# The last down projection of a two-layer encoder step, with tokens as the stationary side of the matmul

## What is computed

```python
def _swiglu(h, wg, wu, wd):
    return (jax.nn.silu(h @ wg) * (h @ wu)) @ wd
...
        h = _rmsnorm(x, prm['ffn_norm'][i, 1])
        x = x + 0.5 * _swiglu(h, prm['ffn_w_gate'][i, 1], prm['ffn_w_up'][i, 1], prm['ffn_w_down'][i, 1])
```

## Time and profile before

| what | value |
|---|---|
| median of 3 runs | 1389.95 us (1389.91 to 1391.57) |
| the profiled execution | 1391.69 us, its span 1390.0 us, mean granted clock 0.998 |
| TensorE with matmuls in flight | 1370.0 us (99%), 10726 matmuls |
| VectorE, ScalarE, GpSimd busy | 865.0 us (62%), 584.2 us (42%), 335.1 us (24%) |
| DMA | 188.34 MB, mean 136 GB/s |

### The profile page before, as it was taken

One profiled execution on the slowest core, in us unless ns is written; L12 is line 12 of the kernel. 1 busy time (PEld: TensorE's weight loads), 2 busy tenths in 40 slices (PEclk: granted clock), 3 DMA queues, 4 the chain that ended last, 5 costly groups with the idle time before them and its releaser, 6 DMA issues.

```text
span 1390.0 us, 27392 instructions
## 1 busy us (share of the span) xinstructions
PE 1370.0 (99%) x10726; PEld 1333.7 (96%) x10726; DVE 865.0 (62%) x1397; ACT 584.2 (42%) x1061; POOL 335.1 (24%) x352
## 2 busy tenths in 40 slices
PE   9999999999999999999999999999999899999998
PEld 8999999999879999999999999998999799999998
DVE  6666646577786666655666655667663667666542
ACT  6333323434765333323433332368544544333321
POOL 4000013766426000022100002456755240000000
PEclk9999999999999999999999999999999999999999
DMA  7655962434522655854455594233333225555661
GB/s 200 183 148 150 275 173 54 120 117 130 160 70 70 173 150 146 224 153 103 124 149 150 151 257 128 60 101 92 93 92 92 91 69 149 151 151 154 166 164 38
DMA packets 324067, 188.34 MB, mean 136 GB/s; under 512 B 10986, under 2 KB 321384, under 8 KB 323996
## 3 DMA queue, kind: packets, MB, share of 16 engines
q1 hardware_dynamic: 322416, 183.23, 48.3%
q0 software_dynamic: 1216, 3.98, 0.9%
q10 hardware_dynamic: 364, 0.15, 0.0%
HBM read 183.22 MB, written 4.11 MB: 135 GB/s over the span
## 4 chain that ended last, share of the span: by engine, by line
PE 92%; DVE 4%; ACT 2%; issue 1%; DMA 0%; ACTq 0%
PE PS L677 22%; PE PS L678 22%; PE PS L679 22%; PE PS L794 3%; PE PS L815 2%; PE PS L796 2%; PE PS L795 2%; PE PS L816 2%; PE PS L817 2%; PE PS L767 1%; PE PS L769 1%; PE PS L768 1%; DVE h_lo L2019 1%; PE PS L1258 1%; PE PS L1277 1%; PE PS L1290 1%
## 5 line engine op out<-in xcount | busy, mean ns | idle before, releaser
L677 PE MATMUL PS<-h_hi,w_parts 128*128 128x320 f32 x1408 | 436.6, 310 | 1.8 <-DVE h_lo L2019 1.1
L679 PE MATMUL PS<-h_hi,w_parts 128*128 128x320 f32 x1408 | 435.1, 309 | 0.0
L678 PE MATMUL PS<-h_lo,w_parts 128*128 128x320 f32 x1408 | 435.1, 309 | 0.0
L677 PEld LDWEIGHTS PS<-h_hi,w_parts 128*128 128x128 f32 x1408 | 264.3, 188 | 3.4 <-DVE h_lo L2019 1.7
L678 PEld LDWEIGHTS PS<-h_lo,w_parts 128*128 128x128 f32 x1408 | 264.4, 188 | 0.3
L679 PEld LDWEIGHTS PS<-h_hi,w_parts 128*128 128x128 f32 x1408 | 264.3, 188 | 0.0
L1434 ACT ACTIVATE w_parts<-gu 128x1024 fp32r<-128x1024 f32 (+1 forms) x178 | 176.9, 1041 | 160.1 <-PE PS L679 155.4
L677 PE MATMUL PS<-act_hi,w_parts 128*128 128x320 f32 x704 | 217.7, 309 | 0.0
L679 PE MATMUL PS<-act_hi,w_parts 128*128 128x320 f32 x704 | 217.5, 309 | 0.0
L678 PE MATMUL PS<-act_lo,w_parts 128*128 128x320 f32 x704 | 217.5, 309 | 0.0
L2007 DVE TENSOR_TENSOR w_parts<-gu,w_parts 128x1024 fp32r<-128x1024 f32 x174 | 206.8, 1230 | 4.0 <-ACT w_parts L1434 3.8
(11 more groups left out here) (383 smaller groups left out, 2191.5 us busy)
## 6 DMA issues: line engine op xcount, KB each, us to landing
dn<-in_ffn_w_down SPq DMA_DIRECT2D x32, 1408.0 KB, 7.0
gu<-in_ffn_w_gate SPq DMA_DIRECT2D x87, 512.0 KB, 4.0
gu<-in_ffn_w_up SPq DMA_DIRECT2D x87, 512.0 KB, 5.2
gu<-in_od_w_in SPq DMA_DIRECT2D x32, 512.0 KB, 4.9
gu<-in_ev_w_in SPq DMA_DIRECT2D x26, 512.0 KB, 4.8
dn<-in_ev_w_out SPq DMA_DIRECT2D x4, 1024.0 KB, 5.8
dn<-in_od_w_out SPq DMA_DIRECT2D x4, 1024.0 KB, 5.4
RB<-bias_rows POOLq DMA_DIRECT2D x2, 576.0 KB, 6.5
```

The source lines that it names most:

```text
L677: mm(out, w_hi, hi, start=first, stop=False)
L678: mm(out, w_hi, lo, start=False, stop=False)
L679: return mm(out, w_lo, hi, start=False, stop=last)
```

## The change

It concerns the last block's down projection and what stands around it.

- In `down_by_tokens`, activations are stationary and weights move: 128 tokens' activations of one k tile by 512 columns of weights. A unit (k, h) is the k tile's rows of the half h of the 1024 output features. The two blocks of 128 prompt tokens take three matmuls each per unit (`block_rows`). The 64 sample tokens' high and low parts lie side by side in 128 columns (`sample_acts`), so that two matmuls do (`sample_rows`), their two halves being added later. The six results fill banks 4 to 7, 0 and 1 and stay there over all 22 k. The loop over pairs of tiles is gone; the code is written out.
- The weights come in 9 groups of 5 units (the last of 4), two slots alternating, loaded by one or two DMAs with rows of 4 KB (a whole k tile) or 2 KB, and split in parts of 3 and 2 units.
- The residual is turned to rows by token inside gate and up: 12 transposes behind `norm` and 12 ahead of `gate_up` 20, there with three more of `rstd`; ScalarE copies them to `ytok`, `ysample` and `ycol` (times 0.25). `turn_out` and `epilogue` go.
- `activate` writes the prompt's and the sample's columns by two instructions each.
- At the end VectorE adds PSUM times `ycol` to the rows, one 128 x 512 block at a time (four of 64 x 512 for the sample), and SP stores each block.

The diff, cut to its core:

```diff
-        ytok = view(RB, 0, 2, D)
-        ysample = hT[:, :, :].rearrange("p k t -> p (k t)")[:, 0:D]
+        sample_acts = rounded("sample_acts", RB_at + high_at, FT * P)
+        y_at = high_at + FT * P
+        ytok = view(RB, y_at, 2, D)
+        ysample = view(RB, y_at + 2 * D, D)
+        ycol = view(RB, y_at + 3 * D, 3)
+        assert y_at + 3 * D + 3 <= RB_N
...
-        def y_bank(part, i):
-            return ((0, 1, 2), (3, 6, 7), (0, 1, 2))[part][i]
+        DN_UNITS = [[(u // 2, u % 2) for u in range(5 * q, min(5 * q + 5, 2 * FT))] for q in range(9)]
+
+        DN_SPLIT = [3] * 8 + [2]
+
+        def unit_halves(q):
+            return slice(0, DN_SPLIT[q] * 512), slice(DN_SPLIT[q] * 512, len(DN_UNITS[q]) * 512)
+
+        def y_bank(i, h):
+
+            return bank(4 + 2 * i + h) if i < 2 else bank(h)
...
+            def load_units(q):
+                n = DN_FFN[3] + q
+                if q < 2:
+                    sp.wait_ge(*dn_free(n - 2))
+                else:
+                    sp.wait_ge(lo_done, halves_before(3, FT + q - 1))
+                w = ffn_w(I["ffn_w_down"], 3)
+                units = DN_UNITS[q]
+                at = 0
+                while at < len(units):
+                    k, h = units[at]
+                    whole = 0 if h else (len(units) - at) // 2
+                    if whole:
+                        sp.dma_start(dn[:, n % 2, at * 512:(at + 2 * whole) * 512].rearrange("p (k c) -> p k c", c=D),
+                                     w[:, k:k + whole, :]).then_inc(dn_loaded[n % 2], 16)
+                        at += 2 * whole
+                    else:
+                        sp.dma_start(dn[:, n % 2, at * 512:(at + 1) * 512], w[:, k, h * 512:(h + 1) * 512])\
+                            .then_inc(dn_loaded[n % 2], 16)
+                        at += 1
...
             y_rows = O["y_prompt"][0].rearrange("(i p) d -> p i d", p=P)
-            for evacs, c0, c1 in ((11, 0, 512), (14, 512, 896)):
-                sp.wait_ge(pro_evac, evacs)
-                store(y_rows[:, :, c0:c1], ytok[:, :, c0:c1])
-                store(O["y_sample"][0][:, c0:c1], ysample[0:TS, c0:c1])
-            sp.wait_ge(pro_evac, 16)
-            store(y_rows[:, :, 896:D], ytok[:, :, 896:D])
+            sp.wait_ge(pro_evac, 19)
+            store(O["y_sample"][0], ysample[0:TS, :])
+            for i in range(2):
+                for h in range(2):
+                    w = slice(h * 512, (h + 1) * 512)
+                    sp.wait_ge(pro_evac, 20 + 2 * i + h)
+                    store(y_rows[:, i, w], ytok[:, i, w])
...
+                if f == 3:
+                    turn_x(0, 0, 4)
+                    turn_x(0, 1, 5)
+                    turn_x(1, 0, 7)
                 gate_up(1, 1, 0)
-                with pe.Fori(1, FT // 2) as i:
+                with pe.Fori(1, FT // 2 - (f == 3)) as i:
                     gate_up(0, 0, i)
                     gate_up(1, 1, i)
+                if f == 3:
+                    pe.wait_ge(norm_rstd, NORM_FFN[3] + 1)
+                    pe.wait_ge(pro_evac, 11)
+                    turn_x(1, 1, 5)
+                    turn_x(2, 0, 4)
+                    turn_x(2, 1, 6)
+                    for i in range(3):
+                        rows = P if i < 2 else TS
+                        ins = tr(bank(7)[0:rows, i * P:(i + 1) * P], rstd[:, i * P:i * P + rows], ident[:, :])
+                    ins.then_inc(pro_pe, 1)
+                    gate_up(0, FT - 2, 0)
+                    gate_up(1, FT - 1, 0)
+                    down_by_tokens()
+                    return
                 down(0, 0, 0)
                 down(1, 1, 0)
-                with pe.Fori(1, KT // 2 - (f == 3)) as i:
+                with pe.Fori(1, KT // 2) as i:
                     down(0, 0, i)
                     down(1, 1, i)
...
+            def turn_x(i, h, b):
+
+                rows = P if i < 2 else TS
+                for k in range(4):
+                    ins = tr(bank(b)[0:rows, k * P:(k + 1) * P], xT[:, 4 * h + k, i * P:i * P + rows], ident[:, :])
+                ins.then_inc(pro_pe, 1)
+
+            def down_by_tokens():
+
+
+                def block_rows(k, h, i):
+                    hi, lo = (a[:, k * T + i * P:k * T + i * P + P] for a in (act_hi, act_lo))
+                    w_hi, w_lo = weights[k, h]
+                    mm(y_bank(i, h), hi, w_hi, start=(k == 0), stop=False)
+                    mm(y_bank(i, h), lo, w_hi, start=False, stop=False)
+                    return mm(y_bank(i, h), hi, w_lo, start=False, stop=(k == FT - 1))
+
+                def sample_rows(k, h):
+
+                    both = sample_acts[:, k * P:(k + 1) * P]
+                    w_hi, w_lo = weights[k, h]
+                    mm(y_bank(2, h), both, w_hi, start=(k == 0), stop=False)
+                    return mm(y_bank(2, h), both, w_lo, start=False, stop=(k == FT - 1))
+
+                weights = {}
+                pe.wait_ge(act_split, FT * 4 + 1)
+                pe.wait_ge(pro_evac, 15)
+                for q, units in enumerate(DN_UNITS):
+                    last = q == len(DN_UNITS) - 1
+                    slot = (DN_FFN[3] + q) % 2
+                    for j, unit in enumerate(units):
+                        weights[unit] = [w_parts[:, slot, part, j * 512:(j + 1) * 512] for part in range(2)]
+                    for j, (k, h) in enumerate(units):
+                        if j in (0, DN_SPLIT[q]):
+                            pe.wait_ge(lo_done, halves_before(3, FT + q) + 1 + (j > 0))
+                        if last:
+                            continue
+                        block_rows(k, h, 0)
+                        block_rows(k, h, 1)
+                        ins = sample_rows(k, h)
+                    if not last:
+                        ins.then_inc(dn_done, 1)
+                pe.wait_ge(act_split, FT * 4 + 2)
+                for h in range(2):
+                    sample_rows(FT - 2, h)
+                    sample_rows(FT - 1, h).then_inc(pro_pe, 1)
+                for i in range(2):
+                    for h in range(2):
+                        block_rows(FT - 2, h, i)
+                        block_rows(FT - 1, h, i).then_inc(pro_pe, 1)
 
...
+            def split_units(q):
+                n = DN_FFN[3] + q
+                loads = 2 * (q // 2 + 1) - (q == len(DN_UNITS) - 1)
+                sc.wait_ge(dn_loaded[n % 2], 16 * (DN_FFN[3] // 2 + loads))
+                if q >= 2:
+                    sc.wait_ge(dn_done, n - 1)
+                else:
+                    sc.wait_ge(gu_done, GU_FFN[3] + FT - 1 + q)
+                for w in unit_halves(q):
+                    copy(w_parts[:, n % 2, 0, w], dn[:, n % 2, w]).then_inc(hi_done, 1)
...
                     split_gate_up(f, 0, 2, i)
                     tanh(1, 1, i)
                     split_gate_up(f, 1, 3, i)
                     tanh(0, 2, i)
+                if f == 3:
+                    x_rows(12, ytok[:, 1, 512:D], bank(5))
+                    x_rows(13, ysample[0:TS, 0:512], bank(4)[0:TS, :])
+                    x_rows(14, ysample[0:TS, 512:D], bank(6)[0:TS, :])
+                    sc.wait_ge(pro_pe, 15)
+                    for i in range(2):
+                        copy(ycol[:, i:i + 1], bank(7)[:, i * P:i * P + 1], 0.25)
+                    copy(ycol[0:TS, 2:3], bank(7)[0:TS, 2 * P:2 * P + 1], 0.25).then_inc(pro_evac, 1)
+                    split_units(0)
+                    tanh(1, FT - 1, 0)
+                    for q in range(1, len(DN_UNITS)):
+                        split_units(q)
+                    return
...
+                        return
                     cols_ = slice(c * T, (c + 1) * T) if type(i) is int else bass.ds(2 * T * i + T * c, T)
                     cp(act_hi[:, cols_], gated[:, slot, :]).then_inc(act_mid, 1)
                     ve.wait_ge(act_mid, mids + 2 + 2 * c + 4 * i)
                     tt(act_lo[:, cols_], gated[:, slot, :], act_hi_32[:, cols_], ALU.subtract).then_inc(act_split, 1)
+
+                def activate_rows(slot, c, i):
+
+
+                    def at(step, start, n_):
+                        return slice(step * c + start, step * c + start + n_) if type(i) is int \
+                            else bass.ds(2 * step * i + step * c + start, n_)
+
+                    prompt, high, low = at(T, 0, TP), at(P, 0, TS), at(P, TS, TS)
+                    sample_32 = sample_acts[:, :].bitcast(F32)
+                    cp(act_hi[:, prompt], gated[:, slot, 0:TP])
+                    cp(sample_acts[:, high], gated[:, slot, TP:T]).then_inc(act_mid, 1)
+                    ve.wait_ge(act_mid, mids + 2 + 2 * c + 4 * i)
+                    tt(act_lo[:, prompt], gated[:, slot, 0:TP], act_hi_32[:, prompt], ALU.subtract)
+                    tt(sample_acts[:, low], gated[:, slot, TP:T], sample_32[:, high], ALU.subtract).then_inc(act_split, 1)
 
...
+                if f == 3:
+                    split_units(0)
```

(60 more changed lines are left out.)

7 lines of the change are left out of this document (4 added, 3 removed).

## The result

Changed kernel: median 1393.72 us of 17 runs (1391.66 to 1394.64), kernel before: 1390.88 us of 17 (1389.9 to 1393.29); ratio 1.0016, interval 1.0009 to 1.0022. By the ratio it is slower by about 2.2 us, within 0.2%. Both kernels' times fall into two groups some 2 us apart (before, nine with a median of 1390.05 and eight with 1392.0; changed, six with 1392.14 and eleven with 1393.95), and as the shares of the groups differ, the medians of all lie 2.8 us apart. The spans of the two profiled executions lie only 0.3 us apart, 1390.3 against 1390.0, and that needs care, so I cut both into stages at products that both have: the first of the odd output projection, of the last gate and up, and of the last down projection.

The account below looks back on a forecast made before the run. TensorE, with matmuls in flight for 99% of the span, was taken as the bound. Stream +2.4, transposes +0.7 and end -1.1 gave +2.0 us on the 1389.95 us median: forecast 1391.9 us, range 1387.8 to 1395.2.

Parts of the forecast that it names:

- The pitch: Time between starts of successive down projection matmuls: 146.7 ns before, 226.7 ns forecast after, making the stream 2.4 us longer.
- Reading (a): Down projection: 13.3 ns surplus belongs to each weight load, so 226.7 ns per product, 79.8 us of stream; chance 0.60.
- (b): Down projection: surplus is a tenth of the columns, stream 82.6 us, +5.2 us, total 1394.7 us; chance 0.15.
- (c): Down projection: surplus vanishes at 512 columns, 216.6 ns per product, stream 76.2 us, -1.2 us, total 1388.3; chance 0.17.
- Transposes: Before, 21 interrupt the down projection; after, 27 in gate/up at 0.109 us take 2.95 us, net +0.7 us.
- Steps at no cost: Start of gate/up, VectorE's work there, weight loads and splits, and written-out code: zero for each.
- ScalarE's six copies: Short copies behind `tanh` 20, before the down projection: 3.3 us at most, first weight half still 2.5 us in hand.
- VectorE's pieces: Gate/up: activation cast and subtraction in two pieces each, at worst +0.82 us per tile, inside idle time, zero cost.
- the new groups: Down projection weights in groups of five units: splits take 4.6 us inside a group's 9.07 us, zero cost.
- the written-out code: Down projection no longer a loop: zero cost, as the odd input projection issues 136 matmuls without a gap.
- Rival (3): Down projection: a group's weights come late, seven groups lose 3.5 us, total 1395.4 us; chance 0.04.
- The end: From the last product's start to the span's end: 5.1 us instead of 6.21, -1.1 us (-0.5 to -1.5).

## Why the prediction was right

**The pitch, the deciding term.** Reading (a) gave 226.7 ns and a stage of 79.6 us; measured were 226.7 and 79.58. (b), 234.7, and (c), 216.6, are out. A surplus that comes once per product, whatever its columns, is borne out by the 256-column run: 12.8 ns for each more product with its load. That it is the load's, the reason given for (a), isn't shown: every product in every run has a load of its own, and neither half the loaded columns nor the same activations twice in a row took anything off. The reading was also too wide in one respect: the surplus belongs to fp32r. For bf16 the pitch of reading (c), 216 ns, is the one measured. The argument against (c), that a load fits into 109 ns, was the weak step: it says nothing about either surplus, and the rows of before, which have no fp32r product of another width, couldn't exclude (c). With a chance of 0.17 for it, the choice of (a) was a likely guess that came true, not a proof.

**Transposes.** 27 by 109 ns, predicted 2.95, measured 2.96, and the fewer-transposes run gave 109 ns each. The 2.30 us that before spent on 21 of them inside the down projection are gone: this is why the stage's total shows no change though its stream grew by 2.4 us.

**Steps at no cost.** ScalarE's six copies (1.70 us against the bound of 3.3), VectorE's pieces, the new groups and the written-out code cost nothing that any stage shows: gate and up grew by the transposes alone, and the down projection has no gap. Rival (3), late weights, didn't occur:

```profile
dn<-in_ffn_w_down SPq DMA_DIRECT2D x9, 1024.0 KB, 5.1
```

**The end.** Predicted 5.1, measured 5.14 us, and the terms hold one by one: 0.43 us to the addition as predicted, 0.75 for it against the 0.68 taken from the earlier trace rows, 0.02 to SP, 2.17 for the last store (2.2 predicted; the median of the four is 3.0, but the earlier ones land before it and don't set the end), and 1.77 behind its landing against the 1.8 carried over.

**The total.** +2.0 predicted, +1.89 by stages, 2.2 by the ratio. The median of 1393.72 is 1.8 us above the 1391.9 of the forecast, and that is the two groups of times: 1391.9 was built on a median of before, 1389.95, that belongs to the lower group, and the lower group of the changed kernel has 1392.1; for an execution like the profiled one the prediction had 1393.7, and the upper group has 1393.95. That 1389.95 equals the profiled span is chance: a time lies 1.7 us above its own span, here 1392.03 against 1390.3.

## What to carry to other kernels

Swapping the stationary and the moving side pays by the number of products saved, each with its load, times the surplus of one, minus the columns added: here 176 x 13.3 ns = 2.3 us against 11,264 columns or 4.7 us, a loss of 2.4, since the 64 sample tokens take two whole products a unit where half of three would be their share. Read that surplus from the distance of starts in a row of the same type; busy sums of TensorE and of its loads say nothing about it (loads fell by 13.7 us here and the stage not at all). A cheaper type helped here only in uniform runs: against 79.58 us in fp32r, the same partly bf16 products cost 82.84 us mixed, 77.85 sorted and 75.19 with neighbouring groups turned towards each other. A narrower load by itself cost 0.8 us.

## What was not expected of the hardware

The surplus depends on the type: 13.3 ns per product with its load for fp32r, 2.5 for bf16, at 512 columns. And at the lower clock the fp32r one isn't there. In the profile of before TensorE's granted clock falls to the 1.2 GHz level for 3.4 us inside the odd mixer; a window (the clock is the third number from the end), and its timeline there:

```profile
933.00:936.00 3.00, 3.00 (x12) 2.99 (x12) 2.19 (x7) 2.37 (x6) 1.29 (x1) 0.50 1.00 314
```

```profile
930.53 2.54 PE L1189 MATMUL PS<-RB,ident 8*128 8x320 f32 x8
...
933.71 0.47 PE L796 MATMUL PS<-h_hi,w_mix 128*128 128x320 f32 x1
933.98 0.47 PE L794 MATMUL PS<-h_hi,w_mix 128*128 128x320 f32 x1
...
941.63 2.42 PE L1189 MATMUL PS<-RB,ident 8*128 8x320 f32 x8
```

At that level fp32r products of 320 columns start 267 ns apart, 320/1.2 = 266.7, with nothing over. The fall comes behind eight matmuls with 8 rows each. In 3.4 us at 267 ns instead of 146.7 it loses 3.4 x (1 - 146.7/267) = 1.5 us. The changed kernel's profile has the same eight matmuls and stays at full clock; the window, and TensorE at the same places:

```profile
930.00:950.00 20.00, 19.77 (x130) 17.20 (x129) 15.29 (x36) 13.16 (x36) 11.01 (x9) 1.00 0.35 106
```

```profile
930.26 2.41 PE L1276 MATMUL PS<-RB,ident 8*128 8x320 f32 x8
...
939.83 2.41 PE L1276 MATMUL PS<-RB,ident 8*128 8x320 f32 x8
...
952.66 0.69 PE L1292 MATMUL PS<-RB 128*64 128x64 f32 x16 [1.68 <-DVE RB L2630]
```

Before is 930.53 - 930.26 = 0.27 us behind ahead of the fall and 941.63 - 939.83 = 1.80 behind it, so the fall cost 1.53; 1.56 are left at the first cut, 1.3 of them the fall's. The second profile of the changed kernel has a fall as well, some 10 us later:

```profile
940.00:946.00 6.00, 6.00 (x24) 5.06 (x24) 5.11 (x12) 2.80 (x6) 1.71 (x2) 0.72 0.51 166
```

```profile
952.56 0.69 PE L1292 MATMUL PS<-RB 128*64 128x64 f32 x16 [0.46 <-DVE RB L2630]
```

This one cost nothing: TensorE waits for VectorE ahead of 952.56, and the fall only took 1.2 us off that wait, 0.46 us in place of 1.68. The odd output projection starts at 1118.37, as early as without a fall (1118.46). Nor does every late profile have one: that of the run with another order within a unit is granted 1.00 from 930 to 950 and starts that projection at 1119.71, and it was 1.25 us late already at 926 us. So the same code meets the fall in some executions and not in others, at a price between nothing and 1.3 us by where it comes. What decides it no run here was made to tell.
